# A two-layer hybrid decoder step: final norm on rows, and a new order at the first loads, gate sums, a head's end and the gate tile

## What is computed

```python
def rmsnorm(x, g):
    r = lax.rsqrt(jnp.mean(x * x, axis=-1, keepdims=True) + EPS)
    return (x * r) * g
# layer 0
h = rmsnorm(x, norm0_g); proj = einsum('btd,de->bte', h, w_in0)      # 7176 columns, the last 8 are gates
x = x + einsum('bte,ed->btd', concat([y_pool, y_mlstm]), w_out0)
# layer 1
h = rmsnorm(x, norm1_g); proj = einsum('btd,de->bte', h, w_in1)      # 48 of the columns are gates
gate = jax.nn.sigmoid((gts + b_gate).astype(f32))
x = x + einsum('bte,ed->btd', (gate-weighted attention) * silu(z), w_out1)
y = rmsnorm(x, final_g)                                              # y_prompt (1,512,2048), y_sample (8,1,2048)
```

## Time and profile before

| | us |
|---|---|
| median of three runs | 2200.79 (2199.15 to 2200.84) |
| the profiled execution | 2201.82 |
| its span, first to last instruction | 2200.0 |
| granted clock of PE, mean | 0.993 |
| PE busy | 2142.8 |

### The profile page before, as it was taken

How to read it: one execution, slowest core, us unless ns; L and a number is a source line. 1 busy time by engine, 2 the same in 40 slices (tenths; PEclk the granted TensorE clock), 3 DMA queues, 4 the chain that set the end, 5 groups by cost and what they waited for, 6 DMA issues and landing times.

```text
span 2200.0 us, 43569 instructions
## 1 busy us (share of the span) xinstructions
PE 2142.8 (97%) x17955; PEld 2037.0 (93%) x17955; DVE 899.0 (41%) x1854; ACT 694.5 (32%) x964; POOL 763.3 (35%) x584
## 2 busy tenths in 40 slices
PE   8999999999999989999999999999999999999995
PEld 7999989989899989999889999899889999889995
DVE  6333135144351361144256533663266434672114
ACT  6211124233231341243234323342234223452221
POOL 2445334424244334444221343124321333023440
PEclk9999999999999999999999999999999999999997
DMA  8333655538465334355635354424535354414431
GB/s 261 89 95 82 192 155 114 181 97 215 135 154 168 92 96 145 109 192 141 163 86 146 83 144 115 135 79 117 157 96 140 82 148 125 119 42 122 116 106 78
DMA packets 454645, 281.13 MB, mean 128 GB/s; under 512 B 19160, under 2 KB 445720, under 8 KB 452659
## 3 DMA queue, kind: packets, MB, share of 16 engines
q1 hardware_dynamic: 454475, 278.73, 45.2%
HBM read 249.87 MB, written 45.99 MB: 134 GB/s over the span
## 4 chain that ended last, share of the span: by engine, by line
PE 50%; issue 30%; POOL 16%; DVE 4%; ACT 0%; POOLq 0%; DVEq 0%; ACTq 0%
PE ps L366 35%; POOL w_lo L344 16%; PE ps L1103 3%; PE ps L1201 2%; PE ps L1176 2%; PE ps L1205 1%; PE ps L1002 1%; PE ps L1137 1%; PE ps L1027 1%; PE ps L1209 1%; DVE xy L1999 1%; PE ps L990 0%; PE ps L1013 0%; PE ps L1229 0%; DVE scratch L1841 0%
## 5 line engine op out<-in xcount | busy, mean ns | idle before, releaser
L344 POOL TENSOR_TENSOR w_lo<-w_raw,w_hi 128x512 fp32r<-128x512 f32 x580 | 763.1, 1348 | 1384.5 <-ACT w_hi L328 1067.0
L366 PE MATMUL ps<-h_hi,w_hi 128*128 128x260 f32 x4640 | 964.0, 289 | 10.7 <-DVE h_lo L458 6.8
L366 PE MATMUL ps<-h_hi,w_lo 128*128 128x260 f32 x4640 | 935.4, 283 | 0.0
L366 PE MATMUL ps<-h_lo,w_hi 128*128 128x260 f32 x4640 | 933.8, 283 | 0.0
L366 PEld LDWEIGHTS ps<-h_hi,w_hi 128*128 128x128 f32 x4640 | 719.9, 189 | 35.0 <-issue 17.7
L366 PEld LDWEIGHTS ps<-h_hi,w_lo 128*128 128x128 f32 x4640 | 715.8, 189 | 0.0
L366 PEld LDWEIGHTS ps<-h_lo,w_hi 128*128 128x128 f32 x4640 | 714.8, 189 | 0.0
L328 ACT ACTIVATE w_hi<-w_raw 128x2048 fp32r<-128x2048 f32 x133 | 254.9, 1917 | 527.4 <-PE ps L366 504.8
L430 DVE TENSOR_TENSOR scratch<-ps,rstd 128x520 f32<-128x520 f32 x48 | 33.6, 700 | 268.2 <-PE ps L366 267.8
L467 DVE TENSOR_TENSOR xy<-ps,x_res 128x520 f32<-128x520 f32 x32 | 22.4, 699 | 257.4 <-PE ps L366 253.8
L1413 ACT ACTIVATE scratch<-ps,scratch 128x128 f32<-128x128 f32 (+3 forms) x128 | 66.4, 524 | 137.3 <-DVE scratch L1870 136.9
(11 more groups left out here) (348 smaller groups left out, 1764.8 us busy)
## 6 DMA issues: line engine op xcount, KB each, us to landing
w_raw<-in_w_in SPq DMA_DIRECT2D x113, 1024.0 KB, 5.8
w_raw<-in_w_out SPq DMA_DIRECT2D x32, 1024.0 KB, 6.1
scratch<-in_cache_kv_sel SPq DMA_DIRECT2D x256, 64.0 KB, 2.0
scratch<-in_cache_kv_win SPq DMA_DIRECT2D x128, 128.0 KB, 2.5
scratch<-in_cache_kv_cmp SPq DMA_DIRECT2D x256, 64.0 KB, 2.0
out_kvw_s<-in_cache_kv_win SPq DMA_DIRECT2D x24, 512.0 KB, 6.6
x_scratch<-xy SPq DMA_DIRECT2D x2, 4160.0 KB, 13.0
x_res<-x_scratch SPq DMA_DIRECT2D x32, 260.0 KB, 6.3
```

What stands on the lines that cost most here:

```text
L344: ins = nc.gpsimd.tensor_tensor(WL[:, t.p, k:k + 4], WR[:, t.p, k:k + 4], WH[:, t.p, k:k + 4].bitcast(F32), ALU.subtract)
L366: mm = nc.tensor.matmul(PS[:, bank + c, 0:HALF], lhsT=w[:, t.p, k, :], rhs=h[:, k, c * HALF:(c + 1) * HALF], start=(k == 0 and x == 0), st ...
```

## The change

- Start: block 0 of x is issued first, then c_common, then the gate columns of w_in0, then the other small loads. ACT splits tile 1's weights in four quarters, behind x tiles 4, 6, 8 and 10. EPS lies in a column of RTOK, and ACT's Sqrt scales and adds; DVE's instruction for it goes.
- Gate sums: the four transposes of AR and the copy move into pooling group 1, in bank 6; the wait for `pl_y` in PE goes. SP still waits for it ahead of the broadcasts.
- A head's end: the Sqrt table, the wait for `m_var` and the root come ahead of the split of the next tile; then Silu once for both gates. In head 3, DVE makes low parts 7 to 10 ahead of the gating multiplies, and ACT splits tile 58 ahead of its high parts 14 and 15.
- Gate tile (73): its weights are split for 48 columns and its matmuls have 48 stationary columns. ACT splits it behind high part 2 of layer 1's input, not ahead of part 0. DVE empties tile 72 behind ten low parts instead of twelve and adds the last squares behind all of them. The split of tile 75 comes ahead of the Sigmoid and its table.
- End: ACT multiplies each finished tile of XY by its gain in place, under the next projection (`weigh`); DVE does so for the last one, into XR. PE turns unscaled tiles in eight banks, five groups before the norm's sums; ten matmuls with one column sum RS and the last squares by row; ACT's Sqrt scales and adds EPS, DVE inverts the 4 + 1 columns, and the copies out of PSUM multiply by them. SP stores half rows (4 KB), eight times.

The diff, without context except where order matters, and dedented by hunk:

```diff
@@ -325,7 +325,8 @@
-nc.scalar.activation(WH[:, t.p], WR[:, t.p], ACT.Copy).then_inc(S["w_hi"], 1); own.done("w_hi")
+n = slice(0, 48 if isinstance(t.n, int) and t.n == G1_BASE else P)
+nc.scalar.activation(WH[:, t.p, :, n], WR[:, t.p, :, n], ACT.Copy).then_inc(S["w_hi"], 1); own.done("w_hi")
@@ -337,12 +338,12 @@
-def split_lo(pool, t):
+def split_lo(pool, t, n=P):
-        ins = nc.gpsimd.tensor_tensor(WL[:, t.p, k:k + 4], WR[:, t.p, k:k + 4],
-                                      WH[:, t.p, k:k + 4].bitcast(F32), ALU.subtract)
+        ins = nc.gpsimd.tensor_tensor(WL[:, t.p, k:k + 4, 0:n], WR[:, t.p, k:k + 4, 0:n],
+                                      WH[:, t.p, k:k + 4, 0:n].bitcast(F32), ALU.subtract)
@@ -363,7 +365,7 @@
-mm = nc.tensor.matmul(PS[:, bank + c, 0:HALF], lhsT=w[:, t.p, k, :],
+mm = nc.tensor.matmul(PS[0:m, bank + c, 0:HALF], lhsT=w[:, t.p, k, 0:m],
@@ -389,7 +391,7 @@
-act.wait_ge(S["nrm_var"], r + 1)
+act.wait_ge(S["nrm_var"], r)
@@ -480,14 +482,16 @@
 add_squares(7, 0)
-for k in range(12 if r == 0 else 0):
+for k in range(10 if r == 0 else 0):
     xg_lo(dve, own, k)
 empty(7, 1)
-for k in range(12, 14 if r == 0 else 0):
+for k in range(10, KT if r == 0 else 0):
     xg_lo(dve, own, k)
-add_squares(7, 1)
-for k in range(14, KT if r == 0 else 0):
-    xg_lo(dve, own, k)
+if r == 0:
+    add_squares(7, 1)
+else:
+    nc.vector.tensor_scalar(XR[:, 0], XY[:, KT - 1], PR[:, R_GF + KT - 1:R_GF + KT], None, ALU.mult
+                            ).then_inc(S["fin_x"], 1); own.done("fin_x")
@@ -496,16 +500,27 @@
     own.done("sq_made")
-with own.turns(7, {"w_hi": 2, "sq_made": 2}) as i:
+def weigh(i, j):
+    y = XY[:, bass.ds(2 * i + j, 1), :]
+    nc.scalar.activation(y, y, ACT.Copy, scale=PR[:, bass.ds(R_GF + 2 * i + j, 1)]
+                         ).then_inc(S["fin_y"], 1)
+    own.done("fin_y")
+with own.turns(7, {"w_hi": 2, "sq_made": 2, **({"fin_y": 2} if r else {})}) as i:
     for j in range(2):
         split_hi(act, own, Tile(base, j, i, 2).ahead(2))
+        if r:
+            weigh(i, j)
 square(7, 0)
+if r:
+    weigh(7, 0)
+    table(own, ACT.Sqrt)
 if r == 0:
-    split_hi(act, own, Tile(base, 0, 7, 2).ahead(2))
     for k in range(14):
         xg_hi(act, own, k)
+        if k == 2:
+            split_hi(act, own, Tile(base, 0, 7, 2).ahead(2))
     split_hi(act, own, Tile(base, 1, 7, 2).ahead(2))
@@ -565,15 +580,15 @@
+load_x(0)
+sp.dma_start(WR[:, 0, :, 0:8], I["w_in0"].rearrange("(k p) n -> p k n", p=P)[:, :, 7168:7176],
+             allow_slow_non_contiguous=True).then_inc(w_loaded[0], 16)
-load_x(0)
-sp.dma_start(WR[:, 0, :, 0:8], I["w_in0"].rearrange("(k p) n -> p k n", p=P)[:, :, 7168:7176],
-             allow_slow_non_contiguous=True).then_inc(w_loaded[0], 16)
@@ -768,13 +783,15 @@
-    sp.wait_ge(S["fin_act"], 2 * i + 2)
-    sp.wait_ge(S["fin_dve"], 2 * i + 2)
-    sp.dma_start(O["y_prompt"][0, i * P:(i + 1) * P], YROW[:, i]).then_inc(S["y_out"], 16)
+    for a in range(2):
+        sp.wait_ge(S["fin_act"], 2 * i + a + 1)
+        sp.wait_ge(S["fin_dve"], 2 * i + a + 1)
+        c = slice(a * 1024, (a + 1) * 1024)
+        sp.dma_start(O["y_prompt"][0, i * P:(i + 1) * P, c], YROW[:, i, c]).then_inc(S["y_out"], 16)
-for name, n in (("y_out", 16 * (NT + 1)), ("row_out", 16 * 44), ("row_first", 64), ("win_out", 16 * 32), ("c_out", 64 * NS),
+for name, n in (("y_out", 16 * (2 * NT + 1)), ("row_out", 16 * 44), ("row_first", 64), ("win_out", 16 * 32), ("c_out", 64 * NS),
@@ -841,6 +858,11 @@
+if g == 1:
+    pe.wait_ge(S["g_dve"], 4)
+    for i in range(NT):
+        mm = T(PS[:, 6, i * 4:(i + 1) * 4], AR[:, i * P:(i + 1) * P], ident[0:4, 0:4])
+    mm.then_inc(S["g_acolT"], 1)
@@ -851,11 +873,6 @@
-pe.wait_ge(S["pl_y"], 8 + 1)
-for i in range(NT):
-    mm = T(PS[:, 4, i * 4:(i + 1) * 4], AR[:, i * P:(i + 1) * P], ident[0:4, 0:4])
-mm.then_inc(S["g_acolT"], 1)
@@ -1216,21 +1233,38 @@
-norm_pe(pe, 2)
-for f in range(20):
+bank_of = (4, 5, 6, 2, 7, 0, 3, 1)
+def turned(f):
-    if i == 0:
-        pe.wait_ge(S["fin_y"], 4 * kk + 4)
-    if f >= 4:
-        pe.wait_ge(S["fin_dve" if f % 2 else "fin_act"], (f - 4) // 2 + 1)
+    if f >= 8:
+        pe.wait_ge(S["fin_dve" if f % 2 else "fin_act"], (f - 8) // 2 + 1)
+        src = XY[:, 4 * kk + k] if 4 * kk + k < KT - 1 else XR[:, 0]
-            mm = T(PS[:, f % 4, k * P:(k + 1) * P], XY[:, 4 * kk + k, i * P:(i + 1) * P], ident)
+            mm = T(PS[:, bank_of[f % 8], k * P:(k + 1) * P], src[:, i * P:(i + 1) * P], ident)
-            mm = T(PS[0:NS, f % 4, k * P:(k + 1) * P], XY[:, 4 * kk + k, TP:TA], ident)
+            mm = T(PS[0:NS, bank_of[f % 8], k * P:(k + 1) * P], src[:, TP:TA], ident)
+pe.wait_ge(S["fin_y"], KT - 1)
+pe.wait_ge(proj_read[0], N_TILES // 2)
+for f in (0, 1, 2, 4, 5):
+    turned(f)
+pe.wait_ge(S["sq_sum"], KT + 2 + 15)
+pe.wait_ge(S["sq_made"], 2 * KT)
+for i in range(NT + 1):
+    n = P if i < NT else NS
+    M(PS[0:n, 1, i:i + 1], lhsT=RS[:, i * P:i * P + n], rhs=ones[:, 0:1], start=True, stop=False)
+    mm = M(PS[0:n, 1, i:i + 1], lhsT=SQS[1][:, 1, i * P:i * P + n], rhs=ones[:, 0:1], start=False, stop=True)
+mm.then_inc(S["nrm_mm"], 1)
+pe.wait_ge(proj_read[1], N_TILES // 2)
+pe.wait_ge(S["fin_x"], 1)
+turned(3)
+turned(6)
+pe.wait_ge(S["nrm_sqrt"], 3)
+for f in range(7, 20):
+    turned(f)
@@ -1253,13 +1287,19 @@
-    if k == 6:
-        split_hi(act, own, Tile(P_BASE, 0))
+    if k % 2 == 0 and 4 <= k < 12:
+        if k == 4:
+            act.wait_ge(w_loaded[1], 16)
+        q = slice(2 * k - 8, 2 * k - 4)
+        ins = A(WH[:, 1, q], WR[:, 1, q], ACT.Copy)
+        if k == 10:
+            ins.then_inc(S["w_hi"], 1); own.done("w_hi")
-act.wait_ge(S["nrm_var"], 1)
-A(RTOK[:, 0:5], RTOK[:, 0:5], ACT.Sqrt).then_inc(S["nrm_sqrt"], 1); own.done("nrm_sqrt")
+act.wait_ge(S["row_sq2"], 2)
+A(RTOK[:, 0:5], RTOK[:, 0:5], ACT.Sqrt, scale=1.0 / D, bias=RTOK[:, 5:6]
+  ).then_inc(S["nrm_sqrt"], 1); own.done("nrm_sqrt")
@@ -1323,38 +1363,37 @@
     t = Tile(M_BASE, 8, h, 10)
+    table(own, ACT.Sqrt)
+    act.wait_ge(S["m_var"], h + 1)
+    A(HRS, HRS, ACT.Sqrt).then_inc(S["m_sqrt"], 1); own.done("m_sqrt")
     split_hi(act, own, t.ahead(2))
     A(S0["kT"][:, 0], S0["kT"][:, 0], ACT.Silu).then_inc(S["gate_on"], 1); own.done("gate_on")
-    table(own, ACT.Sqrt)
-    act.wait_ge(S["m_var"], h + 1)
-    A(HRS, HRS, ACT.Sqrt).then_inc(S["m_sqrt"], 1); own.done("m_sqrt")
     t = Tile(M_BASE, 9, h, 10)
         y_hi(act, own, 0, range(11))
-    table(own, ACT.Silu)
     if h < 3:
 y_hi(act, own, 0, range(11, KT - 2), O0_BASE)
+split_hi(act, own, Tile(M_BASE, 9, 3, 10).ahead(2))
 for j in range(2):
     y_hi(act, own, 0, (KT - 2 + j,), O0_BASE)
-split_hi(act, own, Tile(M_BASE, 9, 3, 10).ahead(2))
 out_act(act, own, 0, O0_BASE)
 t = Tile(G1_BASE, 0)
+split_hi(act, own, t.ahead(2))
 table(own, ACT.Sigmoid)
 A(XR[0:48, 0], XR[0:48, 0], ACT.Sigmoid, bias=S1["bg"][0:48, 0:1]).then_inc(S["g1_sg"], 1); own.done("g1_sg")
-split_hi(act, own, t.ahead(2))
@@ -1448,24 +1487,34 @@
-norm_act(act, own, 2)
+act.wait_ge(S["nrm_mm"], 3)
+rt = S1["cst"][:, 0]
+A(rt[:, 0:4], PS[:, 1, 0:4], ACT.Sqrt, scale=1.0 / D, bias=S1["cst"][:, 1, 0:1])
+A(rt[0:NS, 4:5], PS[0:NS, 1, 4:5], ACT.Sqrt, scale=1.0 / D, bias=S1["cst"][0:NS, 1, 0:1]
+  ).then_inc(S["nrm_sqrt"], 1); own.done("nrm_sqrt")
+act.wait_ge(S["nrm_var"], 2)
-    act.wait_ge(S["fin_T"], f + 1)
+    act.wait_ge(S["fin_T"], (1, 0, 3, 0, 4, 0, 7)[f] if f < 7 else f + 1)
-    A(dst[q, kk * 512:(kk + 1) * 512], PS[q, f % 4, :], ACT.Copy).then_inc(S["fin_act"], 1); own.done("fin_act")
+    A(dst[q, kk * 512:(kk + 1) * 512], PS[q, (4, 5, 6, 2, 7, 0, 3, 1)[f % 8], :], ACT.Copy, scale=rt[q, i:i + 1]).then_inc(S["fin_act"], 1); own.done("fin_act")
-with pool.Fori(0, N_TILES // 2 - 1) as i:
+with pool.Fori(0, G1_BASE // 2 - 1) as i:
+split_lo(pool, Tile(G1_BASE - 1, 0))
+split_lo(pool, Tile(G1_BASE, 0), 48)
+with pool.Fori(0, (N_TILES - A_BASE) // 2) as i:
+    for j in range(2):
+        split_lo(pool, Tile(A_BASE, j, i, 2))
@@ -1489,7 +1538,8 @@
-V.memset(RTOK, 0.0).then_inc(S["gate_on"], 1); own.done("gate_on")
+V.memset(RTOK[:, 0:5], 0.0)
+V.memset(RTOK[:, 5:6], EPS).then_inc(S["gate_on"], 1); own.done("gate_on")
@@ -1510,7 +1560,6 @@
-TS(RTOK[:, 0:5], RTOK[:, 0:5], 1.0 / D, EPS, ALU.mult, ALU.add).then_inc(S["nrm_var"], 1); own.done("nrm_var")
@@ -1578,6 +1627,10 @@
+if g == 1:
+    dve.wait_ge(S["g_acolT"], 1)
+    CP(S0["acol"].rearrange("p (h i) -> p i h", i=NT), PS[:, 6, 0:16].rearrange("p (i h) -> p i h", h=4)
+       ).then_inc(S["g_acol"], 1); own.done("g_acol")
@@ -1587,10 +1640,6 @@
-dve.wait_ge(S["g_acolT"], 1)
-CP(S0["acol"].rearrange("p (h i) -> p i h", i=NT), PS[:, 4, 0:16].rearrange("p (i h) -> p i h", h=4)
-   ).then_inc(S["g_acol"], 1); own.done("g_acol")
-dve.wait_ge(S["g_acol"], 1)
@@ -1714,12 +1763,14 @@
 empty0(dve, Tile(M_BASE, 9, h, 10), kT[:, 1])
+if h == 3:
+    y_lo(dve, own, 0, range(7, 11))
 dve.wait_ge(S["gate_on"], 9 + 4 * h + 4)
 if h == 3:
```

(15 more changed lines are left out.)

## The result

| | before | after |
|---|---|---|
| median, us | 2200.01 (2199.15 to 2200.84, 4 runs) | 2182.22 (2181.45 to 2183.91, 4 runs) |
| the profiled execution / its span | 2201.82 / 2200.0 | 2182.84 / 2181.1 |
| PE busy | 2142.8 | 2136.5 |

The ratio is 0.9926, 95% interval 0.9913 to 0.9938. The forecast was 2173.5 (2168 to 2180). The kernel is faster, but by 9.5 us less than summed, and the time lies 2.2 us above the range.

The account below looks back on a forecast made before the run. PE, busy 97% of the span, was taken as the bound, so only cut waits count. Terms -18.3 + 0 - 1.7 - 2.0 - 5.3 = -27.3 took 2201.82 to 2174.5, median 2173.5 (range 2168 to 2180).

Parts of the forecast that it names:

- Final norm, -18.3: Tail after the last projection: row-side scaling and half-row stores end the span at 2181.7, 18.3 us less (16 to 20).
- First loads, 0: Start: PE begins 4.0 us later, but the first norm's matmuls come at 43.4 against 43.3, so 0 us.
- The bound (+3): Start: up to 3 us lost at the first norm if the hold-up is longer or nothing is recovered.
- not the bytes but SP's queue: Start: the cost of putting block 0 and gate columns first is x_sample's issue held in SP's queue, 4.00 us now.
- Gate sums, -1.7: Gate transposes: moved into the second pooling group, their 1.7 us wait at L857 goes; bounds -0.7 to -2.1.
- Heads 0 to 2, 0: Ends of these heads: the weight split comes 2.6 us later with some 2 us still in hand, so no change.
- Head 3, -2.0: End of head 3: last low halves end at 794.3 instead of 796.3, 2.0 us less; bounds 0 and -6.8.
- Gate tile, -5.3: Layer 1's gate tile with 48 columns: 4.1 us there plus a 1.2 us wait on POOL; bounds -2.5 and -5.7.
- Rival 2: Start loses 3 us with nothing recovered and head 3 gains nothing: 2178.5; chance 17%.
- rival 4: Tail: the eight half stores run one behind the other, deciding from 5 us a piece, total 2200.6 or slower; chance 2%.
- The sum: Whole kernel: the terms add to -27.3 us, giving a forecast median of 2173.5.

Follow-up runs that it names:

- gate-columns-behind kernel: Changed kernel with the gate columns moved behind the small loads, x block 0 still first; 2182.98 us, ratio 0.9930 to the kernel before.
- the tail alone: Kernel before with only the final norm's part of the change; 2180.65 us against 2197.16 for the kernel before beside it, ratio 0.9923.
- set 2: Runs on one chip with the kernel before beside them (2199.20 us); the unedited changed kernel took 2182.30 us there, ratio 0.9925.
- the changed kernel again: Changed kernel without further edits, measured and traced again beside the kernel before; 2182.30 us against 2199.20, ratio 0.9925.
- split behind: Changed kernel with ACT's weight split for the second output projection tile moved behind head 3's sixteenth low half; 2188.45 us, ratio 0.9955 to before.

## Why the prediction was wrong, step by step

- **Final norm, -18.3: right.** 18.2 in the changed kernel and alone, against a tail of before with the longer stretch of half clock; 17.1 against the shorter one. Inside, the twenty one-column passes took 2.0 us (2.4 estimated), roots and reciprocals 0.8, and the store from first issue to the span's end 13.7 instead of 12.9.
- **First loads, 0: wrong, +1.5 in the two traces.** The times up to ACT's last x tile were right (PE at 9.9, ACT's first tile at 14.57, its end at 33.3). What failed is the last line of that step, "through the two row squares, the next split, Sqrt, reciprocal and the diagonal": ACT is 1.7 later at its end (33.3 against 31.6), DVE's instruction was worth 0.1 to 0.2 and not 1.1, since the diagonals take 4.31 us here instead of 3.34, the last one now beside POOL's split, and the wait at the norm's matmul stayed at 0.95, where I had looked for under 0.7. The bound (+3) held. The mechanism was half right: the queue's door holds x_sample, but with the door open the load waits inside ("not the bytes but SP's queue" is refuted by the gate-columns-behind kernel). And the trace of before ran its first gate matmuls at half clock; against a start at full clock the loss is 3.3.
- **Gate sums, -1.7: right** (-1.8); the third tile of head 0 doesn't wait.
- **Heads 0 to 2, 0: the step that failed.** I wrote that the split, 2.6 us later, had 2 us in hand, and gave this no bounds. The 2.6 us are one Sqrt with its table in front of the split; I left out what this Sqrt waits for. In heads 0 to 2 DVE makes the variance behind sixteen state updates, in head 3 the updates come later, and I had looked at head 3's times. It costs 6.4 us, and 7.9 where half clock follows. This alone is most of the 9.5 us that are missing, and shown from both ends.
- **Head 3, -2.0: right** (-2.1, waits of 4.6 left). That DVE's ops with two SBUF inputs and POOL's split hold each other up is shown by moving POOL's split behind and ahead. The Trainium skill states an exclusive lock for this pair (SBUF — State Buffer, "SBUF: two separate sides"). The runs agree that they contend: a low half takes 0.70 us alone and 1.64 to 1.68 beside POOL, one for each of POOL's pieces of 1.7.
- **Gate tile, -5.3: mechanism right, size partly luck.** -4.1 by itself: the waits went, but a new one of 0.7 us came (L990, on DVE's products for the gate), and a part of what I counted was the half clock behind the old wait, 1.3 us (983.98 to 1001.53 is 17.55 us in the first trace of before, 983.85 to 1000.12 is 16.27 with the tail alone), which comes in some executions only.
- **Rivals.** None was it. Rival 2 had the start's loss (3) in it; rival 4's stores run at 400 GB/s and overlap. A rival that stands for a split made late in heads 0 to 2 was missing.
- **The sum** with the shown terms: 18.2 + 1.8 + 2.1 + 4.1 - 6.4 - 3.3 = 16.5, or 15.4 with the old tail's shorter half clock, and 1.3 to 1.8 more against a slow start; measured 16.9 in set 2, and 17.8 in the first.

## What to carry over

When a wait is moved ahead of other work on an in-order engine, the cost is not the moved instruction but everything that its operand stands behind on the engine that makes it: follow that chain in each iteration of the loop that differs, not in the one at hand. In this kernel a small load behind a big one was late whether its issue was held or not, so look at what the first instruction needs before anything goes in front of it. Price a wait, and a start, from more than one execution where the clock may differ, and read the pace of equal matmuls beside the clock column.

## What was not expected of the hardware

- Behind a wait of PE of 1.9 to 2.7 us the granted clock fell to the lower level for a few us in some executions of one program and not in others: behind the first wait in head 0 in three of six traces with that wait (the others are the changed kernel again, split behind, gate columns behind), behind the 2.58 us wait at 1976 in eleven of eighteen traces, behind the 2.7 us wait ahead of output 0 in one of five. Cost 1.1 to 1.5 us where it was measured. The second and third wait of 1.93 us had none in any of the six.
- The first rise of PE's clock came anywhere from 11.87 to 18.05 us, with PE's first instruction at 5.5 or at 9.4 to 10.1, and the profile's clock column doesn't show the time ahead of it. With the old loads it moves the first norm by some 1.5 us. What sets the moment is open.
- POOL's split beside DVE's state updates slows these as well: one takes 0.49 us alone and 1.39 beside a split, and sixteen took 12.85 us where the next split lay beside the last of them (before) and 10.11 where it came behind (changed).
